# Down weights of the experts loaded as two halves of the partitions, two neighbouring rows to a partition

## The chip, the cores and the metric

The kernel runs on one core of a Trainium2 chip. The metric is the device time of one execution in microseconds (us); lower is better. All numbers of a profile are of one profiled execution.

## The reference

One inference step of a two-layer decoder for a prompt group of 256 tokens and a sample group of 64 tokens (320 in all) with D = 1024. Each layer has a token mixer and then a channel mixer. The first layer's channel mixer is a dense SwiGLU; the second's is a mixture of 8 experts, of which each token uses two. The change touches only the experts:

```python
def _swiglu(h, w_gate, w_up, w_down):
    return (jax.nn.silu(h @ w_gate) * (h @ w_up)) @ w_down
...
    for e in range(N_EXPERTS):
        out = out + combine[..., e:e + 1] * _swiglu(h, w_gate[e], w_up[e], w_down[e])
```

`w_gate[e]` and `w_up[e]` are 1024 x 2816, `w_down[e]` is 2816 x 1024, all float32: 34.6 MB an expert, of which the down weights are 11.5 MB.

## The kernel before, in words

The experts' part begins some 1207 us into the span and ends at 2003 us. It is a row of jobs; a job is one expert with up to 64 tokens (narrow) or up to 128 (wide). In the profiled execution there are eight: job 0 narrow, job 1 "both" (one expert with 192 slots), job 2 narrow, job 3 wide, job 4 narrow, job 5 wide, job 6 narrow, job 7 narrow (the jobs' kinds are fixed in the code; how many follow the seventh is read from the routing).

A job works through 35 pairs of weight tiles. Pairs 0 to 23 are gate and up weights (16 pairs of 2 x 512 KB, then 8 of 2 x 384 KB), pairs 24 to 34 are down weights: 11 pairs, each of two tiles of 128 rows of `w_down` (2 x 512 KB, 1.05 MB). The tiles lie in a ring `MRAW` of seven pairs.

SyncE alone issues these loads (`load_job`, line 551): for each pair it waits until TensorE has used the pair seven places before (`m_used`), then issues two DMAs that both count on the slot's semaphore `m_raw`; so up to seven pairs are loading or wait to be used. In the kernel before, a DMA of a down pair brings one tile of 128 rows: partition p gets row 128 kf + p, 4 KB, for all 128 partitions (lines 568 to 571).

TensorE takes a pair when both its DMAs have landed. A narrow job multiplies the raw tiles (line 2999 for gate and up, line 3017 for down). In a wide job ScalarE first makes a rounded copy (line 1893) and VectorE the remainder (line 1200), and TensorE makes three products (lines 2881 to 2887 and 2906 to 2912). The job for both does the wide and the narrow products of the same weights (lines 2937 to 2952 and 2965 to 2980).

The activations (token x 2816) come out of the gate and up products in six pieces, four of 512 columns and two of 384, into the tile `SG`. `turn` (line 2767) transposes each piece in blocks of 128 columns, so that the columns of the piece lie on the partitions, as the down product needs them: block m of a piece is columns 128 m to 128 m + 127. `turn` is called from `side_pe` and `side_both` between the pairs' matmuls.

Of the kernel before, what the change touches and what calls it, by code (L numbers as in the profile page):

```python
# [28 lines left out]
P = 128  # L29
D = 1024  # L30
# [17 lines left out]
HALF = 64  # L48
# [6 lines left out]
GPAIRS = KD * len(GROUPS)  # L55
PAIRS = GPAIRS + KF // 2
HI_RING, RAW_RING = 5, 7
# [45 lines left out]
def tile_at(t):  # L103

    c0, w = GROUPS[t // 2]
    return (c0 + w * (t % 2)) // P, w // P


def slots_of(side, what):
# [147 lines left out]
def build(nc, a, out):  # L257
    ctx = ExitStack()
    with ctx:
# [35 lines left out]
        MRAW = at("mraw", [P, RAW_RING, 2 * D], F32, RING)  # L295
# [136 lines left out]
        PS = ctx.enter_context(nc.psum_tensor("ps", [P, 8, 512], F32))  # L432
        ident = CF[:, C_ID:C_ID + P]
# [3 lines left out]
        for l in range(DEPTH):  # L437
            for p in PARTS:
                src = {"A": a["w_branch_a"], "B": a["w_branch_b"], "O": a["w_out"]}.get(p, a["w_in"])
# [18 lines left out]
        m_raw = [sem(f"m_raw{n}") for n in range(RAW_RING)]  # L458
# [41 lines left out]
        @block.sync  # L500
        def _(sp):
            def load_pause(s, n):

                l, kind = ADA_GROUPS[PAUSE_GROUPS[s]]
                sp.dma_start(PAUSE[s % 2][n][:, :].unsqueeze(1), ada_src[l][:, n:n + 1, kind * D:(kind + 1) * D])\
                    .then_inc(sem(f"pause_in{n // 4}"), 16)

            def load_unit(n):

                kind, what = UNITS[n]  # L510
                if kind == "ada":
                    g, k = what
                    l, part = ADA_GROUPS[g]
                    src = ada_src[l][:, k:k + 1, part * D:(part + 1) * D]
                else:
                    c, part = what
                    if GU_BASE <= c < DOWN_BASE:
                        i, j = (c - GU_BASE) // 2, (c - GU_BASE) % 2
                        src = (gate_src, up_src)[j][:, 4 * part:4 * part + 4, i * CW:(i + 1) * CW]
                    elif DOWN_BASE <= c < DOWN_BASE + 4:  # L520
                        k = c - DOWN_BASE
                        src = down_src[:, 4 * part:min(4 * part + 4, KF), k * CW:(k + 1) * CW]
                    else:
                        l = 0 if c < GU_BASE else 1
                        p, k = PARTS[(c - 70 * l) // 4], c % 70 % 4 if l == 0 else (c - 70) % 4
                        w, c0 = wide[l, p]
                        src = w[:, 4 * part:4 * part + 4, c0 + k * CW:c0 + (k + 1) * CW]
                if n < KD:
                    sp.dma_start(PAUSE[1][n][:, :].unsqueeze(1), src).then_inc(first_in[n], 16)
                    return  # L530
                if n >= KD + RAW_UNITS:
                    sp.wait_ge(unit_used, n - RAW_UNITS + 1)
                sp.dma_start(RAW[:, n % RAW_UNITS, 0:unit_columns(n)].rearrange("p (k n) -> p k n", k=src.shape[1]),
                             src).then_inc(raw_in[n % RAW_UNITS], 16)

            last = (ENDS[BASE[0, "gb"] + 3], ENDS[DOWN_BASE - 1], ENDS[BASE[1, "gb"] + 3])
            xtm = sem("xtm_in")
            sp.dma_start(XTM[:, 0:2, :], a["x_prompt"][0].rearrange("(t p) d -> p t d", p=P)).then_inc(xtm, 16)
            sp.dma_start(XTM[0:TS, 2, :], a["x_sample"].rearrange("s t d -> (s t) d")).then_inc(xtm, 16)
            for n in range(len(UNITS)):  # L540
                load_unit(n)
                for s in range(3):
                    first = last[s] + RAW_UNITS - 1
                    if n == first and s != 1:
                        sp.wait_ge(sem("on_made"), s // 2 + 1)
                    if first <= n < first + 8:
                        load_pause(s, n - first)

            wg, wu, wd = (a[k][0] for k in ("w_exp_gate", "w_exp_up", "w_exp_down"))

            def load_job(job, e, first=False, both=False):
                g = wg[bass.ds(e, 1)].rearrange("e (k p) n -> p (e k) n", p=P)
                u = wu[bass.ds(e, 1)].rearrange("e (k p) n -> p (e k) n", p=P)
                d = wd[bass.ds(e, 1)].rearrange("e (k p) n -> p (e k) n", p=P)
                for n in range(PAIRS):
                    if not (first and n < RAW_RING):
                        sp.wait_ge(m_used, job * PAIRS + (n - RAW_RING + 1))
                    for j in range(2):
                        if both and n < GPAIRS:
                            (c0, w), k = cols_at(n // 4), 2 * (n % 4)  # L560
                            sp.dma_start(MRAW[:, n % RAW_RING, 2 * w * j:2 * w * (j + 1)].rearrange("p (k n) -> p k n", k=2),
                                         (g, u)[j][:, k:k + 2, c0:c0 + w]).then_inc(m_raw[n % RAW_RING], 16)
                            continue
                        if n < GPAIRS:
                            (c0, w), k = GROUPS[n // KD], n % KD
                            src = (g, u)[j][:, k:k + 1, c0:c0 + 2 * w]
                        else:
                            w, kf = 512, 2 * (n - GPAIRS) + j
                            src = d[:, kf:kf + 1, :]
                        sp.dma_start(MRAW[:, n % RAW_RING, 2 * w * j:2 * w * (j + 1)].unsqueeze(1),  # L570
                                     src).then_inc(m_raw[n % RAW_RING], 16)
                    if first and n == RAW_RING - 1:
                        for i, t in enumerate(HM_TILES):
                            rows = P if t < 2 else TS
                            sp.wait_ge(sem("hm0_out"), i + 1)
                            sp.wait_ge(sem("hm1_out"), i + 1)
                            sp.dma_start(HD[1 + P * t:1 + P * t + rows, :], HMF[0:rows, t, :]).then_inc(hd_stored, 16)

            sp.wait_ge(unit_used, len(UNITS))
            sp.wait_ge(psum_out, CHUNKS)  # L580
            load_job(0, 0, first=True)
            sp.wait_ge(sem("routed"), 1)
            e = sp.value_load(XI[0:1, 1:2], min_val=0, max_val=NE - 1)
            load_job(1, e, both=True)
            with sp.Fori(2, MAIN) as job:
                e = sp.value_load(XI[0:1, bass.ds(job, 1)], min_val=0, max_val=NE - 1)
                load_job(job, e)
            extra = sp.value_load(XI[0:1, 15:16], min_val=1, max_val=1 + EXTRA)
            with sp.Fori(0, 1 + EXTRA) as k:
                with sp.If(k < extra):  # L590
                    e = sp.value_load(XI[0:1, bass.ds(k + MAIN, 1)], min_val=0, max_val=NE - 1)
                    load_job(k + MAIN, e)
            for t in range(2):
                sp.wait_ge(sem("y_out"), 2 * t + 2)
                sp.dma_start(out["yp"][0, P * t:P * t + P, :], XTM[:, t, :]).then_inc(sem("y_stored"), 16)
            sp.wait_ge(sem("y_out"), 2 * TT)
            sp.dma_start(out["ys"].rearrange("s t d -> (s t) d"), XTM[0:TS, 2, :]).then_inc(sem("y_stored"), 16)
            sp.wait_ge(sem("y_stored"), 48)
# [1572 lines left out]
        def _(pe):  # L2171
            M = nc.tensor
# [189 lines left out]
            for d in range(KD):  # L2362
                ins = M.transpose(PS[:, b, d * 16:d * 16 + SEQS], CT[:, d * P:(d + 1) * P], CF[0:SEQS, C_ID:C_ID + SEQS])
# [3 lines left out]
            for k in range(5):  # L2367
                b = aux()
                if k < 4:
                    for d in range(4):  # L2370
                        kd = 4 * (k % 2) + d
                        ins = M.transpose(PS[:, b, d * P:(d + 1) * P], XTM[:, k // 2, kd * P:(kd + 1) * P], ident)
                else:
                    for d in range(KD):
                        ins = M.transpose(PS[:, b, d * TS:(d + 1) * TS], XTM[0:TS, 2, d * P:(d + 1) * P],
                                          CF[0:TS, C_ID:C_ID + TS])
# [23 lines left out]
            for l in range(DEPTH):  # L2400
# [53 lines left out]
                for k in range(4):  # L2454
                    tokens(H1, l)(BASE[l, "i"] + k, k % 2, k)
                    if k == 1:
                        pe.wait_ge(sem("ws_in"), 16 * 10 * (l + 1))
                        b = aux()
                        for g in range(G4):
                            ins = M.transpose(PS[:, b, g * P:(g + 1) * P], WSRR[:, g, :], ident)  # L2460
# [3 lines left out]
                for g in range(G4):  # L2464
                    ins = M.transpose(PS[:, b, g * P:(g + 1) * P], WSR[:, g, :], ident)
                ins.then_inc(aux_in, 1)
                b = aux()
                for g in range(G4):
                    ins = M.transpose(PS[0:TS, b, g * TS:(g + 1) * TS], WSRS[:, g, :], CF[0:TS, C_ID:C_ID + TS])
                ins.then_inc(aux_in, 1)  # L2470

                for k in range(4):
# [8 lines left out]
                    for m in range(2):  # L2481
                        n = 2 * k + m
# [284 lines left out]
            def turn(bank, src, nf):  # L2767

                for m in range(nf):
                    ins = M.transpose(PS[:, bank, m * P:(m + 1) * P], src[:, m * P:(m + 1) * P], ident)  # L2770
                return ins

            def place(bank, marks):
# [314 lines left out]
```

## Time and profile before

| what | value |
|---|---|
| median of 3 runs | 2020.82 us (2020.23 to 2024.37) |
| the profiled execution's own time | 2022.59 us |
| its span, first to last instruction | 2020.7 us |
| TensorE matmul busy | 1908.5 us, 94% |
| VectorE, ScalarE busy | 962.1 us, 741.7 us |
| SyncE's DMA queue | 458.02 MB, 64.1% of 16 DMA engines' span |
| down weights | 176 DMAs of 512 KB, median 12.3 us from issue to landing |

The busy shares are means over stages with different limits: in some of them TensorE never stops, in others it stands still between pairs until a transfer lands. "DMA share" in the windows is the mean busy share of the 16 DMA engines, and GB/s is what they moved; a share can read a little over 1. A transfer that keeps the engines busy and moves few bytes is limited somewhere other than in the number of engines.

### The profile page before, as it was taken

How to read it: one execution, taken by the hardware profiler on the slowest of the kernel's cores; microseconds unless marked ns; L12 is line 12 of the kernel's file. 1: busy time of each engine (PE TensorE's matmuls, PEld its weight loads, DVE VectorE, ACT ScalarE, POOL GpSimd, SP SyncE). 2: the span in 40 equal slices, each digit the busy share in tenths (PEclk: the TensorE clock that was granted, in tenths of full speed). 3: DMA queues.
4: the chain of work that ended last, by engine and by line, in shares of the span. 5: the costliest groups of instructions: out<-in, count | busy, mean ns of one | idle time of the engine just before them, and what ended most of it. 6: DMA issues, size and time to landing. Idle time of an engine off the chain costs nothing. (4 is left out here: it accounts for less than half of the span.)

```text
span 2020.7 us, 31287 instructions
## 1 busy us (share of the span) xinstructions
PE 1908.5 (94%) x12597; PEld 1480.7 (73%) x12597; DVE 962.1 (48%) x1334; ACT 741.7 (37%) x927; POOL 127.0 (6%) x169
## 2 busy tenths in 40 slices
PE   7999999998999989999999988999998999899797
PEld 5999999997999979999998963456534863584233
DVE  4476554556344354765445451355414751783011
ACT  4434324435334344343244331344304641561001
POOL 2100002300000011000022010000000000000000
PEclk9999999999999999999999989999999999999999
DMA  9635356573665636344565459956699899999995
GB/s 356 203 112 164 113 165 181 187 261 94 199 217 194 199 119 201 94 130 126 186 180 166 158 190 408 376 176 230 211 383 406 300 409 407 374 348 407 400 407 233
DMA packets 239096, 488.48 MB, mean 242 GB/s; under 512 B 16919, under 2 KB 145033, under 8 KB 238962
## 3 DMA queue, kind: packets, MB, share of 16 engines
q1 hardware_dynamic: 229504, 458.02, 64.1%
q0 software_dynamic: 9440, 28.50, 4.6%
q8 instruction: 100, 1.64, 0.3%
q14 instruction: 34, 0.28, 0.0%
q10 hardware_dynamic: 18, 0.04, 0.0%
HBM read 473.90 MB, written 12.59 MB: 241 GB/s over the span
## 5 line engine op out<-in xcount | busy, mean ns | idle before, releaser
L614 DVE TENSOR_TENSOR wlo<-raw,whi 128x1024 fp32r<-128x1024 f32 x244 | 289.1, 1212 | 313.5 <-ACT whi L1602 312.3
L2267 PE MATMUL ps<-h1h,whi 128*128 128x320 f32 x1248 | 386.3, 322 | 7.6 <-DVE h1l L721 3.9
L2268 PE MATMUL ps<-h1l,whi 128*128 128x320 f32 x1248 | 371.7, 310 | 0.0
L1602 ACT ACTIVATE whi<-raw 128x1024 fp32r<-128x1024 f32 x244 | 247.8, 1046 | 119.4 <-PE ps L2652 44.8
L2267 PEld LDWEIGHTS ps<-h1h,whi 128*128 128x128 f32 x1248 | 236.2, 189 | 23.7 <-issue 17.2
L2268 PEld LDWEIGHTS ps<-h1l,whi 128*128 128x128 f32 x1248 | 236.4, 189 | 0.1
L2999 PE MATMUL ps<-mraw,xef 128*64 128x512 f32 (+1 forms) x960 | 211.4, 573 | 17.7 <-DMA mraw<-in_w_exp_up 14.7
L2313 PE MATMUL ps<-h1h,wlo 128*128 128x320 f32 x1248 | 209.3, 310 | 0.0
L2313 PEld LDWEIGHTS ps<-h1h,wlo 128*128 128x128 f32 x1248 | 189.0, 188 | 0.4 <-issue 0.4
L1200 DVE TENSOR_TENSOR mlo<-mraw,mhi 128x2048 fp32r<-128x2048 f32 (+1 forms) x70 | 150.1, 2165 | 9.4 <-ACT mhi L1893 9.3
L2999 PEld LDWEIGHTS ps<-mraw,xef 128*64 128x64 f32 x960 | 62.8, 138 | 122.1 <-issue 87.2
L1893 ACT ACTIVATE mhi<-mraw 128x2048 fp32r<-128x2048 f32 (+1 forms) x70 | 127.1, 1820 | 56.3 <-DMA mraw<-in_w_exp_up 29.0
L3017 PE MATMUL ps<-mraw,gtf 128*64 128x512 f32 x440 | 105.7, 604 | 22.2 <-DMA mraw<-in_w_exp_down 20.8
L1224 DVE TENSOR_TENSOR mhi<-mraw,mhi 128x2048 fp32r<-128x2048 f32 (+1 forms) x35 | 75.9, 2169 | 56.8 <-PE ps L2952 32.1
L3017 PEld LDWEIGHTS ps<-mraw,gtf 128*64 128x64 f32 x440 | 27.1, 136 | 87.2 <-DMA mraw<-in_w_exp_down 53.3
L1422 DVE TENSOR_TENSOR gtf<-sgt,ps 128x256 f32<-128x256 f32 (+1 forms) x36 | 14.3, 398 | 157.3 <-ACT sgt L1941 157.3
L1901 ACT ACTIVATE mhi<-mraw 128x2048 fp32r<-128x2048 f32 (+1 forms) x35 | 63.5, 1815 | 68.8 <-PE ps L2952 42.5
L2881 PE MATMUL ps<-mhi,xeh 128*128 128x512 f32 (+1 forms) x192 | 75.5, 393 | 5.5 <-ACT mhi L1893 5.5
L2267 PE MATMUL ps<-h2h,whi 128*128 128x320 f32 x256 | 77.0, 315 | 0.0
L2268 PE MATMUL ps<-h2l,whi 128*128 128x320 f32 x256 | 75.5, 309 | 0.0
L2882 PE MATMUL ps<-mhi,xel 128*128 128x512 f32 (+1 forms) x192 | 72.5, 378 | 0.0
L2005 ACT ACTIVATE sg<-ps 128x512 f32<-128x512 f32 (+1 forms) x30 | 16.9, 562 | 148.9 <-PE ps L2999 148.9
(489 smaller groups left out, 3017.2 us busy)
## 6 DMA issues: line engine op xcount, KB each, us to landing
mraw<-in_w_exp_down SPq DMA_DIRECT2D x176, 512.0 KB, 12.3
raw<-in_w_in SPq DMA_DIRECT2D x128, 512.0 KB, 4.0
mraw<-in_w_exp_gate SPq DMA_DIRECT2D x128, 512.0 KB, 7.0
mraw<-in_w_exp_up SPq DMA_DIRECT2D x128, 512.0 KB, 8.7
raw<-in_w_ada SPq DMA_DIRECT2D x64, 512.0 KB, 3.8
mraw<-in_w_exp_gate SPq DMA_DIRECT2D x64, 384.0 KB, 6.1
mraw<-in_w_exp_up SPq DMA_DIRECT2D x64, 384.0 KB, 8.0
pause<-in_w_ada SPq DMA_DIRECT2D x32, 512.0 KB, 6.4
```

What stands on the lines that cost most here:

```text
L614: V.tensor_tensor(WLO[:, u % RAW_UNITS, 0:w], RAW[:, u % RAW_UNITS, 0:w], WHI[:, h % HI_UNITS, 0:w].bitcast(F32), ALU.subtract).then_inc(l ...
L1200: V.tensor_tensor(MLO[:, n % RAW_RING, 0:w], MRAW[:, n % RAW_RING, 0:w], MHI[:, n % HI_RING, 0:w].bitcast(F32), ALU.subtract).then_inc(m_l ...
L1224: V.tensor_tensor(MHI[:, BOTH_HI + n % BOTH_LO, 0:w], MRAW[:, n % RAW_RING, 0:w], MHI[:, n % BOTH_HI, 0:w].bitcast(F32), ALU.subtract).the ...
L1602: A.activation(WHI[:, h % HI_UNITS, 0:w], RAW[:, u % RAW_UNITS, 0:w], ACT.Copy).then_inc(hi_made, 1)
L1893: A.activation(MHI[:, n % HI_RING, 0:w], MRAW[:, n % RAW_RING, 0:w], ACT.Copy).then_inc(m_hi, 1)
L2267: M.matmul(out_, w, v[0], start=start, stop=False, skip_group_check=True)
L2268: M.matmul(out_, w, v[1], start=False, stop=False, skip_group_check=True)
L2313: ins = M.matmul(PS[:, 2 * j + m, 0:T], w[1][:, s], parts[0][:, k * T:(k + 1) * T], start=False, stop=(k == KD - 1), skip_group_check=True)
L2881: M.matmul(o_, XEH[:, k, :], hi_[:, s], start=(k == 0), stop=False)
L2882: M.matmul(o_, XEL[:, k, :], hi_[:, s], start=False, stop=False)
L2999: ins = M.matmul(PS[HALF * j:HALF * j + HALF, GROUP_BANKS[g][2 * i], 0:w], XEF[:, k, :], MRAW[:, p % RAW_RING, s], start=(k == 0), stop=(k ...
L3017: ins = M.matmul(PS[HALF * h:HALF * h + HALF, DOWN_BANKS[0], :], GTF[:, kf, :], MRAW[:, p % RAW_RING, s], start=(kf == 0), stop=(kf == KF ...
```

## The change

The rows of the down weights are dealt out to the partitions in another order. A group is what one piece of the activations covers: 512 rows (384 in the last two). Of a group, partition p now takes the four (three) neighbouring rows 4p to 4p + 3 (3p to 3p + 2); tile m of the group is row 4p + m on partition p. Two tiles of a pair that lie in one group are thus two neighbouring rows, 8 KB in one piece, on each partition.

Such a pair is still loaded by two DMAs of 512 KB, but each now covers 64 partitions and both tiles: the first partitions 0 to 63, the second partitions 64 to 127. This holds for 10 of the 11 down pairs. The other pair (tiles 18 and 19) lies across two groups and is loaded as before by two DMAs of 128 partitions x 4 KB, now from rows three apart.

`turn` takes every fourth (third) column of the piece for a block, to match. The number of DMAs, of transposes and of matmuls is unchanged, and so are the ring and all waits.

```diff
+def row_of(kf):
+
+    t = kf // 4 if kf < 16 else 4 + (kf - 16) // 3
+    f0, nf = tile_at(t)
+    return f0 * P, nf, kf - f0
...
+            def load_down(e, n, slot, j):
+
+                kf = 2 * (n - GPAIRS)
+                c0, nf, m = row_of(kf)
+                if row_of(kf + 1)[0] == c0:
+                    rows, part = wd[bass.ds(e, 1), c0:c0 + nf * P, :].rearrange("e (p m) n -> p (e m) n", m=nf), slice(HALF * j, HALF * j + HALF)
+                    sp.dma_start(MRAW[part, slot, :].rearrange("p (m n) -> p m n", m=2), rows[part, m:m + 2, :])\
+                        .then_inc(m_raw[slot], 16)
+                    return
+                c0, nf, m = row_of(kf + j)
+                rows = wd[bass.ds(e, 1), c0:c0 + nf * P, :].rearrange("e (p m) n -> p (e m) n", m=nf)
+                sp.dma_start(MRAW[:, slot, D * j:D * (j + 1)].unsqueeze(1), rows[:, m:m + 1, :]).then_inc(m_raw[slot], 16)
...
-                d = wd[bass.ds(e, 1)].rearrange("e (k p) n -> p (e k) n", p=P)
...
-                            w, kf = 512, 2 * (n - GPAIRS) + j
-                            src = d[:, kf:kf + 1, :]
+                            load_down(e, n, n % RAW_RING, j)
+                            continue
...
-                    ins = M.transpose(PS[:, bank, m * P:(m + 1) * P], src[:, m * P:(m + 1) * P], ident)
+                    ins = M.transpose(PS[:, bank, m * P:(m + 1) * P], src[:, m:nf * P:nf], ident)
```

On SyncE, the end of the first job's loads, in the kernel before (`128x1024` is partitions x elements of one DMA; L570 issues all loads of a job):

```order
L570 DMA mraw<-in_w_exp_gate 128x768
L570 DMA mraw<-in_w_exp_up 128x768
L570 DMA mraw<-in_w_exp_down 128x1024 x22
L583 TENSOR_LOAD xi
L583 ISA x2
```

The same place in the changed kernel (L589 is the old L570, L564 and L569 are the two branches of `load_down`):

```order
L589 DMA mraw<-in_w_exp_gate 128x768
L589 DMA mraw<-in_w_exp_up 128x768
L564 DMA mraw<-in_w_exp_down 64x2048 x18
L569 DMA mraw<-in_w_exp_down 128x1024 x2
L564 DMA mraw<-in_w_exp_down 64x2048 x2
L602 TENSOR_LOAD xi
L602 ISA x2
```

Nothing moved: 22 DMAs stand where 22 stood, and 20 of them have half the partitions and twice the bytes on each. On TensorE the order of all instructions is the same; only the read pattern of the transposes differs.

## Rows read from the trace of the kernel before

**Rows 1.** The page: busy tenths of TensorE and DMA, GB/s, in 40 equal slices.
```profile
PE   7999999998999989999999988999998999899797
...
DMA  9635356573665636344565459956699899999995
GB/s 356 203 112 164 113 165 181 187 261 94 199 217 194 199 119 201 94 130 126 186 180 166 158 190 408 376 176 230 211 383 406 300 409 407 374 348 407 400 407 233
```

**Rows 2.** Stages of the jobs: window, us, busy, granted clock, DMA share, GB/s.
```profile
core 0: us, PE busy (x) PEld busy (x) DVE busy (x) ACT busy (x) POOL busy (x), PEclk, DMA share, GB/s
1257.50:1285.00 27.50, 23.38 (x102) 6.73 (x102) 2.09 (x4) 1.86 (x4) 0.00 (x0) 1.00 1.03 406
...
1403.80:1458.60 54.80, 54.80 (x236) 31.00 (x238) 24.21 (x13) 19.10 (x15) 0.00 (x0) 1.00 0.62 214
1458.60:1512.70 54.10, 51.91 (x249) 19.66 (x249) 9.27 (x23) 6.35 (x13) 0.95 (x1) 1.00 0.95 358
...
1544.00:1616.10 72.10, 71.01 (x330) 58.03 (x331) 59.49 (x49) 47.28 (x34) 0.94 (x1) 0.98 0.91 330
1616.10:1648.20 32.10, 32.04 (x149) 25.83 (x147) 26.02 (x15) 20.32 (x16) 0.00 (x0) 1.00 1.03 410
1648.20:1697.60 49.40, 48.24 (x234) 17.25 (x233) 8.61 (x22) 5.78 (x12) 0.94 (x1) 1.00 1.03 406
1698.60:1726.20 27.60, 23.45 (x102) 6.80 (x102) 2.09 (x4) 1.86 (x4) 0.00 (x0) 1.00 1.03 409
1728.90:1800.80 71.90, 70.81 (x330) 58.11 (x331) 61.29 (x49) 48.15 (x34) 0.95 (x1) 0.98 0.92 341
...
1915.70:1971.30 55.60, 51.05 (x233) 17.27 (x233) 7.89 (x20) 4.81 (x11) 0.00 (x0) 0.97 1.03 407
1972.30:2002.70 30.40, 28.84 (x142) 12.84 (x142) 0.71 (x2) 1.43 (x4) 0.00 (x0) 1.00 0.79 315
```

**Rows 3.** TensorE in order of time, in a narrow job's down stage.
```profile
1892.69 1.94 PE L3017 MATMUL ps<-mraw,gtf 128*64 128x512 f32 x8 [0.61 <-DMA mraw<-in_w_exp_down]
1894.56 0.55 PE L2770 MATMUL ps<-cf,sg 128*128 128x128 f32 x3
1895.26 1.94 PE L3017 MATMUL ps<-mraw,gtf 128*64 128x512 f32 x8 [0.15 <-DMA mraw<-in_w_exp_down]
```

**Rows 4.** The page's costliest groups: busy us, mean ns, idle before and releaser.
```profile
L3017 PE MATMUL ps<-mraw,gtf 128*64 128x512 f32 x440 | 105.7, 604 | 22.2 <-DMA mraw<-in_w_exp_down 20.8
...
L3017 PEld LDWEIGHTS ps<-mraw,gtf 128*64 128x64 f32 x440 | 27.1, 136 | 87.2 <-DMA mraw<-in_w_exp_down 53.3
```

**Rows 5.** Windows around transfers at the span's two ends, columns as in rows 2.
```profile
2015.70:2018.20 2.50, 0.00 (x0) 0.00 (x0) 1.71 (x3) 0.00 (x0) 0.00 (x0) 0.50 1.00 403
...
2018.60:2019.60 1.00, 0.00 (x0) 0.00 (x0) 0.00 (x0) 0.00 (x0) 0.00 (x0) 0.50 1.09 238
5.60:8.00 2.40, 2.33 (x11) 2.33 (x12) 0.00 (x0) 1.69 (x2) 0.39 (x6) 1.00 1.02 247
```

**Rows 6.** DMA issues of the whole span: count, KB each, median us to landing.
```profile
mraw<-in_w_exp_down SPq DMA_DIRECT2D x176, 512.0 KB, 12.3
...
out_yp<-xtm SPq DMA_DIRECT2D x2, 512.0 KB, 2.7
...
xtm<-in_x_sample SPq DMA_DIRECT2D x1, 256.0 KB, 7.3
...
out_ys<-xtm SPq DMA_DIRECT2D x1, 256.0 KB, 2.9
```

**Rows 7.** TensorE in order of time, at the start of wide job 3.
```profile
1544.02 0.47 PE L2881 MATMUL ps<-mhi,xeh 128*128 128x512 f32 x1 [2.74 <-ACT mhi L1893]
1544.33 0.39 PE L2882 MATMUL ps<-mhi,xel 128*128 128x512 f32 x1
...
1547.11 0.63 PE L2881 MATMUL ps<-mhi,xeh 128*128 128x512 f32 x1
```

**Rows 8.** Weight loads of the transposes (line 2770): duration ns min/median/max.
```profile
L2770 PEld LDWEIGHTS ps<-cf,sg x198: 137/140/145, 1226.2 to 1982.0; 128*128 128x128 f32 x198
```

## The prediction

> **What bounds the kernel now.** I read the page's slices first, then the windows of each job's stages, then TensorE in order of time within one stage, and last the transfers elsewhere in the program that look like the new ones. The slices show two halves of the program: up to slice 23 the DMA engines are half idle, and in the last 17 most slices run at 370 to 409 GB/s [rows 1]. That last part is the experts, and only there does the change act.
>
> The windows divide it [rows 2]. In the down stage of a narrow job (1257.5, 1698.6; 27.5 us for 11 pairs) the DMA share is 1.03 at 406 to 409 GB/s, while TensorE is busy for 23.4 us. In order of time a pair is eight matmuls in 1.94 us, and one follows the other after 2.56 or 2.57 us (1892.69, 1895.26), with the wait ended by the landing of down weights [rows 3]. 1.0486 MB at 409 GB/s is 2.56 us as well: transfers set this pace. The wait stands in the group of line 3017 too, 53.3 us of its weight loads' idle time and 20.8 us of its matmuls' [rows 4]. So narrow down stages are bound by transfers, and whatever a down transfer gains or loses comes through there. The gate stages of narrow jobs are nearly bound by them too: share 1.03 in 1648.2 and 1915.7, 0.95 in job 2's [rows 2]. Wide jobs are bound by TensorE, by little: 32.1 us for 11 down pairs are 2.92 us each against 2.56, and the gate stages' share is 0.91 and 0.92. Only the job for both has real room: 54.8 us for 11 pairs are 4.98 us each, at a share of 0.62.
>
> **The change, the loads.** Neither the bytes nor the number of DMAs changes. What changes is that 20 of the 22 DMAs of a job write 64 partitions instead of 128. The trace holds three transfers to set beside each other. At the end of the span two stores of 128 partitions (y of the prompt, 512 KB each) run at share 1.00 and 403 GB/s. Right behind them one store of 64 partitions (y of the samples, 256 KB), with nothing beside it, has the share 1.09 and 238 GB/s [rows 5]; it takes 2.9 us to land where 512 KB take 2.7 [rows 6]. The engines are as busy and move about half. Near the start the load of the samples (64 partitions, 256 KB) lies in a window with share 1.02 and 247 GB/s [rows 5], though other small loads share that window; so it is no matter of stores alone. All 16 engines work on a transfer of 64 partitions, each at half its rate, as if two of them shared one way into the memory.
>
> The price: per unit of share the lone store moves 238 / 1.09 = 218 GB/s. A DMA of 524 KB at that rate takes 2.40 us, a pair of two 4.81 us instead of 2.56 us. Both ends: 247 GB/s gives 4.25 us. At the other end, if two DMAs of opposite halves that stand behind each other in the queue could fill each other's gaps, the pair costs 2.56 us and nothing is lost. I take 4.81: each engine must finish its share of the lower half before it starts on the upper, all 16 start together, and the store is the only row with nothing beside it. The extra is 2.25 us a pair and 22.5 us for the ten pairs of a job.
>
> The Trainium skill has a rule that bears on the two halves together, which no row here shows ("SBUF — State Buffer", section "Can I just issue two DMAs to hit both halves?"): two concurrent DMAs, one at partition 0 and one at partition 64, were only 6% faster than a single one, "they serialize". The table of the section before it ("Door 1: The DMA port swizzle") gives 196 GB/s for partitions 0 to 63; an estimate by that figure is 5.35 us a pair and a sum some 40 us larger than mine. The rows' 238 and 218 GB/s agree in kind.
>
> **The sum over the jobs.** Where transfers set the pace the whole 22.5 us is felt; where the DMA engines stood idle before, that idle time is used up first. Idle time is 1 minus share / 1.03.
> Job 0 (narrow, transfers bind): 22.5.
> Job 1 (both): 4.81 us a pair is below TensorE's 4.98: 0. The cover is thin; at 5.35 us it would cost 4 us.
> Job 2 (narrow behind the one for both): share 0.95 over 54.1 us leaves 4.2 us: 22.5 - 4.2 = 18.3.
> Jobs 3 and 5 (wide): share 0.91 over 72.1 us leaves 8.4, share 0.92 over 71.9 us leaves 7.7: 14.1 and 14.8. Part of it falls into the next job's gate stage, as the ring is then empty instead of full.
> Jobs 4 and 6 (narrow behind wide, share 1.03 throughout): 22.5 each.
> Job 7 (last, narrow): its down stage was 30.4 us with share 0.79, as TensorE's work at the end set 2.9 us of it: 22.5 - 2.9 = 19.6.
> Sum: 134.3 us.
>
> **The clock.** In narrow down stages TensorE will work 1.94 of 4.81 us. At job 3's start an idle stretch of 2.74 us was followed by matmuls of 0.63 us where they had taken 0.39 [rows 7], and the stage's mean granted clock is 0.98 [rows 2], so 0.02 x 72.1 = 1.4 us of it is the price of one such start. At half the clock (1.2 instead of 2.4 GHz) a down pair would take up to 3.9 us, still below 4.81, so within the stage it is hidden. The start of the next stage pays once; two of the five already do. I put 3 us, between 0 and 7 (five starts by 1.4).
>
> **The change, the transposes.** The same 198 weight loads of 140 ns [rows 8] now read every fourth or third column. No row shows such a load. Below: 0, as the count is the same and they lie beside matmuls. Above: each takes twice as long, and matters only where TensorE binds: jobs 3 and 5 have 22 each and job 1 has 44, so 88 x 0.14 = 12.3 us. In narrow jobs it would vanish in the waits. The row nearest is the 140 ns of the plain load; I take 0.
>
> SyncE issues the same number of DMAs behind the same waits, and ScalarE, VectorE and TensorE read the same places of the ring, at no cost.
>
> **Total.** 134.3 + 3 = 137 us. The profiled execution took 2022.6 us, so it would be 2160; the median of the runs is 1.8 us below it, so 2158 us. With both upper ends of clock and transposes it is 2174, and with a rate 10% lower (5.3 us a pair) near 2195.
>
> **Rivals.**
> *The halves slip against each other.* If of two engines that share a way one runs ahead by half a transfer, each is alone half of the time: (2.56 + 4.81) / 2 = 3.69 us a pair, 11.3 us a job. Less the same idle times: 11.3 + 0 + 7.1 + 2.9 + 11.3 + 3.6 + 11.3 + 8.4 = 56 us, so 2077 us. For it: the queue is never empty in these stages, so a lead once gained can last. Against it: a pair of tiles is ready only when the slowest engine is done, and an engine that has caught up waits for the next issue, where all start together again.
>
> *Full rate, and the longer pieces help (the other side).* The place is the same ten pairs. If lower and upper halves overlap fully, nothing is lost, and a partition's 8 KB in one piece could carry less overhead. The best rate over 2 us or more in the rows is 410 GB/s against 406 to 409 in the narrow stages [rows 2]; even 3% would be 0.08 us a pair, 4 us for the 50 pairs of the five narrow jobs and some 1 us in the wide ones: 2016 us, between 2012 and 2021. It decides from the point where a pair of halves takes less than 2.56 us. Against it stands the lone store at 238 GB/s. The Trainium skill speaks for it ("Perfetto Trace Analysis", section "DMA Optimizations"): putting small transfers together into larger ones, its examples go up to 8 KB, is its first advice where transfers bind. No row here shows a piece of 8 KB, and the 4 KB pieces run at 409 GB/s already.
>
> *The change does not do what it says.* If the 8 KB pieces are cut into 4 KB again, only the halving of the partitions is left; the forecast stays.
>
> **How the numbers follow.** The forecast with its unknown costs (2115 to 2195) gets 0.76; the slipping halves (2040 to 2115) 0.12; full rate 0.11; what I have not thought of 0.01. The range 2070 to 2195 leaves out full rate and the lower part of the slipping halves, some 2 in 10 with the misses at the top. A difference under 0.2% (4 us) can't be told from none: the full rate splits into faster 0.06 and same 0.05. Slower has 0.89.
>
> **What would show it.** Right: narrow down stages (27.5 us before) last near 50 us, with a DMA share still near 1.03 and GB/s near 225; the down DMAs' time to landing roughly doubles; the job for both keeps its 54.8 us; wide down stages grow to about 40 us; the transposes' loads stay at 140 ns. Gate stages keep 406 to 409 GB/s wherever gate weights alone are moving. Wrong: a down stage at 400 GB/s or more (full rate), or near 300 with stages of about 40 us (slipping halves); or the job for both longer by more than a few us, or loads of the transposes near 280 ns.

## The result, and the profile after

The changed kernel takes 2193.7 us (median of 4 runs, 2180.04 to 2200.43) against 2022.12 us before (4 runs): ratio 1.0837, 95% interval [1.0795, 1.0878]. The forecast was 2158 us in a range of 2070 to 2195, so the direction and the main mechanism came true and the size was some 35 us short. The median lies 1.3 us under the upper end of the range, and two of the four runs (2195.67 and 2200.43 us) lie above it. The profiled execution took 2191.74 us, its span is 2189.9 us.

The slices of the page after, to set against [rows 1]:

```profile
PE   7999999999999899999998869999698868986776
...
DMA  9634456736666463346654897698999999899995
GB/s 339 213 96 150 146 181 193 241 97 197 198 203 199 129 183 105 112 139 182 199 193 170 329 245 251 173 240 331 238 339 241 360 289 321 255 316 343 309 333 145
```

A slice is now 54.7 us long instead of 50.5. The first 22 slices are the part ahead of the experts, which did not change. Behind them the DMA engines are as busy as before, but slices at 238 to 255 GB/s stand between those at 289 to 360. The windows of the stages say which they are (columns as in [rows 2]; for each job the gate stage and the down stage):

```profile
1208.10:1261.50 53.40, 47.46 (x231) 18.91 (x231) 8.38 (x39) 6.63 (x13) 1.91 (x2) 0.97 0.95 347
1263.10:1313.20 50.10, 32.09 (x102) 8.48 (x102) 2.09 (x4) 1.86 (x4) 0.00 (x0) 0.80 1.02 245
...
1432.40:1487.20 54.80, 54.80 (x236) 31.18 (x236) 24.21 (x13) 19.11 (x15) 0.00 (x0) 1.00 0.87 239
1487.20:1542.20 55.00, 52.27 (x250) 20.27 (x249) 9.27 (x23) 6.35 (x13) 0.95 (x1) 1.00 0.95 338
1545.00:1595.20 50.20, 32.72 (x102) 8.21 (x102) 2.09 (x4) 1.86 (x4) 0.00 (x0) 0.77 1.01 246
1597.90:1670.00 72.10, 71.87 (x329) 58.75 (x329) 58.29 (x47) 45.51 (x32) 0.95 (x1) 0.96 0.91 302
1670.30:1720.20 49.90, 39.07 (x147) 27.30 (x148) 27.67 (x16) 21.68 (x18) 0.00 (x0) 0.93 1.01 258
1720.20:1777.00 56.80, 49.85 (x234) 17.38 (x233) 8.62 (x22) 5.77 (x12) 0.95 (x1) 1.00 1.03 384
1779.90:1828.70 48.80, 33.95 (x102) 8.67 (x102) 2.09 (x4) 1.86 (x4) 0.00 (x0) 0.72 1.02 255
1831.40:1904.40 73.00, 72.47 (x329) 59.14 (x329) 58.29 (x47) 45.48 (x33) 0.95 (x1) 0.95 0.89 294
1904.40:1952.50 48.10, 39.20 (x149) 27.41 (x149) 27.67 (x16) 21.68 (x18) 0.00 (x0) 0.93 1.01 261
...
2017.40:2063.10 45.70, 28.83 (x102) 7.91 (x102) 0.71 (x2) 1.43 (x4) 0.00 (x0) 0.85 1.01 260
2063.50:2124.90 61.40, 52.56 (x233) 17.82 (x233) 7.91 (x20) 5.03 (x11) 0.00 (x0) 0.95 1.03 370
2126.20:2171.40 45.20, 34.29 (x142) 13.97 (x142) 0.71 (x2) 1.43 (x4) 0.00 (x0) 0.89 0.83 194
```

A narrow down stage takes 45.7 to 50.2 us instead of 27.5, at a DMA share of 1.01 to 1.02 and 245 to 260 GB/s (the last job's, which was 30.4 us long, takes 45.2). A wide one takes 49.9 and 48.1 us instead of 32.1 and 31.7. The job for both keeps its 54.8 us; only its share rose from 0.62 to 0.87. In order of time, TensorE in job 2's down stage (compare [rows 3]):

```profile
1544.99 3.63 PE L3036 MATMUL ps<-mraw,gtf 128*64 128x512 f32 x8 [2.74 <-DMA mraw<-in_w_exp_down]
1549.56 1.94 PE L3036 MATMUL ps<-mraw,gtf 128*64 128x512 f32 x8 [0.94 <-DMA mraw<-in_w_exp_down]
1554.11 2.54 PE L3036 MATMUL ps<-mraw,gtf 128*64 128x512 f32 x8 [2.61 <-DMA mraw<-in_w_exp_down]
1556.58 0.91 PE L2789 MATMUL ps<-cf,sg 128*128 128x128 f32 x3
1558.66 3.64 PE L3036 MATMUL ps<-mraw,gtf 128*64 128x512 f32 x8 [1.16 <-DMA mraw<-in_w_exp_down]
```

A pair now follows after 4.55 to 4.57 us instead of 2.56. Some pairs take 3.6 us instead of 1.94 at a lower clock (the stage's mean granted clock is 0.77), still within that time. The groups of the page after, to set against [rows 4], and the down weights' time to landing against [rows 6]:

```profile
L3036 PE MATMUL ps<-mraw,gtf 128*64 128x512 f32 x440 | 142.0, 781 | 89.0 <-DMA mraw<-in_w_exp_down 89.0
...
L3036 PEld LDWEIGHTS ps<-mraw,gtf 128*64 128x64 f32 x440 | 31.8, 160 | 176.5 <-DMA mraw<-in_w_exp_down 131.0
...
mraw<-in_w_exp_down SPq DMA_DIRECT2D x176, 512.0 KB, 22.1
```

The wait for down weights is 89.0 us before the matmuls where it was 20.8, and landing takes 22.1 us where it took 12.3. The transposes' weight loads did get slower: 209 ns where [rows 8] had 140.

```profile
L2789 PEld LDWEIGHTS ps<-cf,sg x198: 188/209/230, 1227.2 to 2141.5; 128*128 128x128 f32 x198
```

### The profile page after: what moved, and what is told of

It is laid out like the page before. It is cut to its first block, busy times and chain, and to the rows that moved or that the text cites. A ratio compares the mean times of both kernels' runs of the same rounds, so it can differ in the third digit from the quotient of the medians.

```text
span 2189.9 us, 31287 instructions
## 1 busy us (share of the span) xinstructions
PE 1974.1 (90%) x12597; PEld 1496.2 (68%) x12597; DVE 962.8 (44%) x1334; ACT 741.3 (34%) x927; POOL 127.3 (6%) x169
## 3 DMA queue, kind: packets, MB, share of 16 engines
q1 hardware_dynamic: 219264, 458.02, 67.4%
## 4 chain that ended last, share of the span: by engine, by line
PE 25%; DMA 21%; DVE 1%; issue 1%; ACT 1%; SPq 1%; DVEq 0%; ACTq 0%
DMA mraw<-in_w_exp_down 14%; DMA mraw<-in_w_exp_up 6%; PE ps L3018 5%; PE ps L2956 2%; PE ps L2900 2%; PE ps L2906 2%; PE ps L2901 2%; PE ps L3036 1%; PE ps L2964 1%; PE ps L2286 1%; PE ps L2984 1%; PE ps L2965 1%; PE ps L2287 1%; PE ps L2971 1%; PE ps L2332 1%
## 5 line engine op out<-in xcount | busy, mean ns | idle before, releaser
L3036 PE MATMUL ps<-mraw,gtf 128*64 128x512 f32 x440 | 142.0, 781 | 89.0 <-DMA mraw<-in_w_exp_down 89.0
L3036 PEld LDWEIGHTS ps<-mraw,gtf 128*64 128x64 f32 x440 | 31.8, 160 | 176.5 <-DMA mraw<-in_w_exp_down 131.0
## 6 DMA issues: line engine op xcount, KB each, us to landing
mraw<-in_w_exp_down SPq DMA_DIRECT2D x176, 512.0 KB, 22.1
```

The costliest lines, as they stand in the source:

```text
L3036: ins = M.matmul(PS[HALF * h:HALF * h + HALF, DOWN_BANKS[0], :], GTF[:, kf, :], MRAW[:, p % RAW_RING, s], start=(kf == 0), stop=(kf == KF ...
```

## The experiments

Two theories of the loss stood against each other first. W: 64 neighbouring partitions are reached by half as many ways as 128, so two DMA engines share one. P: it is the new pieces (8 KB long, or 12 and 16 KB apart from one partition to the next) that read slowly. A third, N, came with e4: any DMA of 64 partitions is slow, whichever they are. The four kernels below ran on one chip, beside the kernel before at 2023.05 us.

**e1, the new order of rows without the halves.**

```diff
-                if row_of(kf + 1)[0] == c0:
+                if False:
```

> New order of rows and transposes as in the changed kernel, but every down DMA covers 128 partitions x 4 KB (rows three or four apart). Theory W (64 neighbouring partitions are reached by half as many ways, two DMA engines share one): the whole loss is gone, narrow down stages 27.5 us at 409 GB/s; what is left is the slower weight loads of the transposes (209 instead of 140 ns, 88 of them where TensorE binds, 6 us): 2020 to 2030 us. Theory P (the pieces' distance of 12 or 16 KB slows the reads): near 2190 us.

2023.43 us, ratio 0.9997 [0.9985, 1.0009]. The first narrow down stage:

```profile
1259.70:1287.20 27.50, 23.51 (x102) 7.01 (x102) 2.09 (x4) 1.86 (x4) 0.00 (x0) 1.00 1.03 406
```

Order and distance of the rows cost nothing that shows: the interval is -3 to +2 us. Nor do the slower weight loads, which this kernel has as well (median 208 ns): the 6 us expected of them did not show in the total.

**e2, one DMA of 128 partitions x 8 KB.**

```diff
-                    rows, part = wd[bass.ds(e, 1), c0:c0 + nf * P, :].rearrange("e (p m) n -> p (e m) n", m=nf), slice(HALF * j, HALF * j + HALF)
-                    sp.dma_start(MRAW[part, slot, :].rearrange("p (m n) -> p m n", m=2), rows[part, m:m + 2, :])\
-                        .then_inc(m_raw[slot], 16)
+                    rows = wd[bass.ds(e, 1), c0:c0 + nf * P, :].rearrange("e (p m) n -> p (e m) n", m=nf)
+                    if j:
+                        return
+                    sp.dma_start(MRAW[:, slot, :].rearrange("p (m n) -> p m n", m=2), rows[:, m:m + 2, :])\
+                        .then_inc(m_raw[slot], 32)
```

> As the changed kernel, but a pair in one group is one DMA of 1 MB, 128 partitions x 8 KB, that counts 32. Theory W: no loss, 2015 to 2030 us, down stages at 409 to 420 GB/s; pieces of 8 KB may gain up to 3% of the down transfers (4 to 5 us against the kernel with 4 KB pieces). Theory P (pieces of 8 KB or their distance are slow): near 2190 us.

2018.76 us, ratio 0.9981 [0.9969, 0.9993]: the whole loss is gone, and there is a gain of some 4 us, close to the noise. Two windows inside narrow down stages (the stages last 26.9 us):

```profile
1253.50:1279.50 26.00, 22.61 (x102) 6.82 (x98) 2.09 (x4) 1.86 (x4) 0.00 (x0) 1.00 1.02 415
1509.00:1535.00 26.00, 22.62 (x102) 6.83 (x98) 2.09 (x4) 1.86 (x4) 0.00 (x0) 1.00 1.01 418
```

**e3, halves alone.** The kernel before with its own order of rows and its own transposes; only the split of a down pair is the new one, in pieces of 4 KB.

```diff
-                            w, kf = 512, 2 * (n - GPAIRS) + j
-                            src = d[:, kf:kf + 1, :]
+                            kf, part = 2 * (n - GPAIRS), slice(HALF * j, HALF * j + HALF)
+                            sp.dma_start(MRAW[part, n % RAW_RING, :].rearrange("p (k n) -> p k n", k=2),
+                                         d[part, kf:kf + 2, :]).then_inc(m_raw[n % RAW_RING], 16)
+                            continue
```

> The kernel before with its old order of rows and plain transposes; only the split of a down pair changes: two DMAs of 64 partitions (0 to 63, 64 to 127) x two pieces of 4 KB, for all 11 pairs. Theory W: slow as the changed kernel, 2175 to 2215 us (11 pairs instead of 10, no slower weight loads). Theory P: 2020 to 2025 us.

2191.04 us, ratio 1.0851 [1.0823, 1.0879]. The halves alone make the whole loss:

```profile
1257.70:1306.00 48.30, 31.80 (x102) 8.22 (x102) 2.09 (x4) 1.86 (x4) 0.00 (x0) 0.79 1.03 237
```

**e4, 64 partitions, but every second one.**

```diff
-                    rows, part = wd[bass.ds(e, 1), c0:c0 + nf * P, :].rearrange("e (p m) n -> p (e m) n", m=nf), slice(HALF * j, HALF * j + HALF)
+                    rows, part = wd[bass.ds(e, 1), c0:c0 + nf * P, :].rearrange("e (p m) n -> p (e m) n", m=nf), slice(j, P, 2)
```

> As the changed kernel (two DMAs of 64 partitions x 8 KB), but the first takes the even partitions and the second the odd ones. Theory W (it matters which partitions a DMA writes, since only neighbouring 64 crowd onto half the ways): all or nearly all of the loss is gone, 2015 to 2040 us. Rival N (any DMA of 64 partitions is slow, whichever they are): near 2190 us.

2018.11 us, ratio 0.998 [0.9967, 0.9994]. The number of DMAs is that of the changed kernel, each is again 64 partitions x 8 KB, and the stage runs at full rate (a window inside a stage of 27.0 us):

```profile
1259.50:1285.50 26.00, 22.52 (x102) 6.82 (x98) 2.09 (x4) 1.85 (x4) 0.00 (x0) 1.00 1.02 414
```

So it is not how many partitions a DMA writes but which: theory N falls, W holds in each of the four. That the shared thing is a way from two engines into the same partitions is the explanation that fits; what the runs show is the dependence on the set of partitions.

The pieces of the transfers say it directly. The trace has a duration for each, and a piece of 8 KB takes 576 ns in the changed kernel (median) and 309 ns in e4.

One thing changes along with the partitions in e4: its DMAs read rows spread over 2 MB of memory, those of the changed kernel rows within 1 MB. No run changes the partitions alone. A theory that blames the narrower stretch of memory has the kernel before against it, whose DMAs read 0.5 MB in one stretch at 406 to 409 GB/s, and e3, whose halves read two such stretches of 0.25 MB each and are slow.

The second four ask for the 35 us that the sum was short. They ran on another chip, beside the kernel before at 2025.31 us. Theory "credit" is the prediction's: the DMA engines' idle time is used up first. Its rival is "full price": that idle time is there because the ring is full, and the lead of seven pairs is what the next job already lives on.

**e5 and e6, halves only in the wide, or only in the narrow jobs.**

```diff
-                if row_of(kf + 1)[0] == c0:
+                if halves and row_of(kf + 1)[0] == c0:
...
-            with sp.Fori(2, MAIN) as job:
-                e = sp.value_load(XI[0:1, bass.ds(job, 1)], min_val=0, max_val=NE - 1)
-                load_job(job, e)
+            for job in range(2, MAIN):
+                e = sp.value_load(XI[0:1, job:job + 1], min_val=0, max_val=NE - 1)
+                load_job(job, e, halves=(job % 2 == 1))
```

(for e6 `== 0`, and the first and last jobs too; the rest of the edit hands `halves` on to `load_down`. The loop over jobs is written out for it on SyncE. No run has that alone; in e5 the narrow down stages without halves last 27.5 to 27.6 us, as before.)

> Of the changed kernel's half-partition DMAs only those of the wide jobs 3 and 5 are left; all other down DMAs cover 128 partitions x 4 KB. Credit theory (the prediction's sum: the idle time of the DMA engines in the gate stage before is used up first): 14.1 + 14.8 = 29 us over the kernel before, about 2052 us. Rival, full price (that idle time is there because the ring of seven pairs is full, and the next job already lives on those seven): 2 x 22.5 = 45 us and a few for the clock, about 2068 to 2074 us.

> Only the narrow jobs 0, 2, 4, 6 and 7 have half-partition DMAs. Credit theory: 22.5 + 18.3 + 22.5 + 22.5 + 19.6 = 105 us, about 2128 us. Full price: 5 x 22.5 - 2.9 = 110 us, and with a clock cost above the 3 us forecast some 10 us more, 2133 to 2145 us. If narrow and wide jobs add up, this one's loss and that of the run with wide jobs alone make the changed kernel's 170 us, less what the two share.

e5: 2066.24 us, ratio 1.0219 [1.0194, 1.0245], 41 us over the kernel before (some 5 us either way): near the 45 of full price, clear of the 29 of credit. Job 3 and the narrow job behind it, in e5:

```profile
1539.00:1612.10 73.10, 72.17 (x329) 59.11 (x330) 58.70 (x48) 46.32 (x33) 0.94 (x1) 0.95 0.93 315
1612.10:1659.40 47.30, 36.59 (x150) 24.98 (x148) 27.50 (x16) 21.18 (x16) 0.00 (x0) 1.00 1.01 258
1659.40:1714.60 55.20, 49.93 (x234) 17.36 (x233) 8.61 (x22) 5.77 (x12) 0.94 (x1) 1.00 1.03 407
```

The gate stage's share is 0.93 where [rows 2] has 0.91: the idle time was hardly used. The down stage is 15.2 us longer, and the gate stage behind it 5.8 us, although its own transfers run at 407 GB/s: it starts without its lead. Together 21 us for one wide job, against 14 with credit. What SyncE waits for during the wide gate stage, in the kernel before (1544 to 1616.1) and in the changed one (1597.9 to 1670):

```profile
SPq L570 <- PE ps L2887: 47.5, 22, 9.0
...
SPq L589 <- PE ps L2906: 42.2, 17, 8.8
```

That is 47.5 and 42.2 us of waiting until TensorE has used a pair, which is a full ring.

e6: 2139.35 us, ratio 1.0563 [1.0534, 1.0592], 114 us over the kernel before, between full price's 110 and 120. The two add up to 155 us of the changed kernel's 164 on this chip; with some 5 us of uncertainty in each of the three, the 9 us that are missing are not clear of noise.

**e7, filler for the clock, and e8, the changed kernel once more.** Behind the down pairs stand matmuls whose result nobody reads, so that TensorE does not stand idle:

```diff
+                    if GPAIRS + 4 <= p < PAIRS - 1:
+                        warm(4, 1)
...
+                    if GPAIRS <= p < PAIRS - 1 and not by_marks and side is not SIDE_FIRST:
+                        warm(5, 1)
```

(first the wide jobs, then the narrow ones)

> The changed kernel with work that has no use for TensorE behind each down pair: five matmuls of 128x320 (1.6 us) in the narrow jobs but the first and the last, four in the last pairs of wide jobs. They fit into the waits for transfers. Theory C (the low clock after those waits costs 12 to 15 us in the stages behind them, instead of the 3 us forecast): granted clock back to 0.98, 8 to 14 us faster than the changed kernel, 2180 to 2186 us. Rival (the clock costs what was forecast): within 3 us of the changed kernel, or slower by the filler.

> The changed kernel once more, as the measure for the others on this chip: 2180 to 2200 us, a granted clock near 0.96.

e7: 2193.96 us, ratio 1.0845 [1.0819, 1.0872]; e8: 2189.26 us, 1.0795 [1.077, 1.082]. The mean granted clock rose from 0.955 (e8) to 0.974 (e7), and the time did not fall. Job 4 of e7, gate and down stage:

```profile
1725.20:1776.30 51.10, 48.48 (x234) 17.84 (x233) 8.62 (x22) 5.78 (x12) 0.94 (x1) 1.00 1.03 387
1779.20:1831.80 52.60, 52.56 (x202) 25.55 (x202) 2.09 (x4) 1.86 (x4) 0.00 (x0) 0.97 1.02 258
```

and of e8:

```profile
1717.50:1775.50 58.00, 50.60 (x234) 17.41 (x233) 8.61 (x22) 5.77 (x12) 0.94 (x1) 0.99 1.03 384
1778.10:1825.70 47.60, 31.24 (x102) 8.24 (x102) 2.09 (x4) 1.85 (x4) 0.00 (x0) 0.79 1.01 238
```

With filler the gate stage is 6.9 us shorter, but it began 7.7 us later, and both end within 1 us of each other (1776.3 and 1775.5), at a DMA share of 1.03. In the down stage the filler takes TensorE to 52.56 us busy of 52.6 and the stage is 5 us longer: there it has become a load of its own. In the profiled executions (2195.6 and 2195.5 us) the three narrow down stages with filler are 12 us longer together than in e8, and the rest of the program is as much shorter, so the total can't say what the clock costs. It shows only that keeping TensorE busy in this way gains nothing.

The stages that TensorE binds say more. A lower clock can cost time where TensorE is busy throughout. The wide gate stages are such stages (71.87 us busy of 72.1), and they come right behind the slow narrow down stages. In the changed kernel they take 72.1 and 73.0 us at a granted clock of 0.96 and 0.95, where they took 72.1 and 71.9 at 0.98 [rows 2]; the gate stage of the job for both takes 117.5 us instead of 117.1. That is 1 to 2 us in all.

## Why the prediction was right, and where it was short

*What bounds.* Right. Down stages bound by transfers took the loss, the job for both hid it: 171.8 us before, 172.3 after.

*The rate of the halves.* Right within some per cent, and this is the step that carried the forecast. The lone store of 64 partitions gave 4.81 us a pair, an extra of 2.25. The page's queue line gives nearly the same afterwards:

```profile
q1 hardware_dynamic: 219264, 458.02, 67.4%
```

67.4% of 2189.9 us are 1476 us; before it was 64.1% of 2020.7, 1295 us. The 181 us more, over 80 pairs, are 2.26 us a pair. Not all of it is in the pairs themselves. The pieces of 8 KB add up to 4.57 us a pair (365.2 us of all 16 engines' time for the 80 pairs, against 207.9 in e4), which is near the 4.55 us between pairs; a piece takes 1.86 times as long, not twice. Another 14 us are in the experts' pieces of 4 KB, which e4 moves in 308.8 us and the changed kernel in 322.8. Why a half takes less than double, and why its neighbours take longer, no run shows. As a forecast of the total the rival of slipping halves (2077 us) is out, and full rate (2016 us) is near what e2 and e4 measured (2019 and 2018 us) once the neighbouring halves were gone.

*The sum over the jobs.* Here it failed: "where the DMA engines stood idle before, that idle time is used up first". For that idle time it took off 4.2, 8.4 and 7.7 us, and 2.9 us in job 7. Measured in the profiled executions, from the first matmul of a job to that of the next (job 7: to its last):

| job | before | after | more | forecast |
|---|---|---|---|---|
| 0 narrow | 79.5 | 106.8 | 27.3 | 22.5 |
| 1 both | 171.8 | 172.3 | 0.5 | 0 |
| 2 narrow | 85.5 | 110.7 | 25.2 | 18.3 |
| 3 wide | 104.1 | 122.3 | 18.2 | 14.1 |
| 4 narrow | 80.7 | 111.2 | 30.5 | 22.5 |
| 5 wide | 103.5 | 121.0 | 17.5 | 14.8 |
| 6 narrow | 83.3 | 111.0 | 27.7 | 22.5 |
| 7 narrow | 87.0 | 107.9 | 20.9 | 19.6 |

Sum 167.8 us against 134.3. The wide gate stages kept their idle time (share 0.91 and 0.89 after, 0.91 and 0.92 before), since SyncE waits there for a place in the ring and can't load further ahead; e5 shows it alone. Job 2's gate stage kept its own as well (share 0.95 before and after), and its 25.2 us stand against a forecast of 18.3. Job 7's 2.9 us rest on something else, TensorE's work at the end, and 20.9 against 19.6 does not speak against them. The prediction's signs show the fault too: it expected wide down stages of about 40 us, and they took 49.9 and 48.1. With nothing taken off the sum is 157.5 us.

Of the 10 us left, the trace accounts for most. Added up over all transfers, the DMA engines are busy 164 us longer in the seven jobs other than job 1, which is 7 us more than seven times 22.5. Their idle time in these jobs grew by 3 us, where the sum had counted on 23 us less of it. Part of the idle time may be at the starts of narrow down stages, where TensorE now waits up to 2.9 us behind the gate stage (1777.0 to 1779.9) where it waited 1.0; that link is not shown.

*The range.* That it held is partly luck. Its upper end came from a rate 10% lower, which is not what happened, and with the upper ends of clock and transposes added on top it would have been some 2212 us. The other rate that the prediction names, 5.35 us a pair, would have come nearer in the total (some 2198 us) with a pair time further off than 4.81 is from the 4.55 measured.

*The clock.* 3 us were put down. The granted clock fell to 0.72 to 0.80 in the first three narrow down stages and to 0.85 and 0.89 in the last two, and it is hidden there, as said. Where TensorE binds, 1 to 2 us show, within the forecast's 0 to 7.

*The transposes.* The sign was wrong, since each load took 209 ns and not 140. The cost of 0 was right for the total, by e1. The last job's down stage, which TensorE's own work lengthens, took 32.0 us in e1's profile and 31.8 in e2's and e4's, where the kernel before has 30.4; that these 1.5 us come from the loads is not shown.

## What to carry to other kernels

Before splitting a load in two, look at which partitions each part covers: stages with DMAs of 64 neighbouring partitions ran at 237 to 260 GB/s where 128 partitions, or every second of them, ran at 406 to 418. A single small transfer of the same shape elsewhere in the trace, with its DMA share beside its GB/s, gave the rate beforehand (4.81 us a pair against 4.57). And idle time of a queue in front of a full ring is no reserve: the lead that the ring holds is already part of the next stage's time, and here none of it came off the cost.

## What was not expected of the hardware

Weight loads of a transpose whose columns stand three or four elements apart took 208 to 209 ns (median) instead of 140, at no cost that shows in the total. Pieces of 8 KB instead of 4 KB took a narrow down stage from 27.5 to 26.9 us in the first four of e2's five narrow jobs, and e2 and e4, whose common difference from e1 is the length of the pieces, are the fastest kernels of this study, 0.2% below the one before. The Trainium skill ("Perfetto Trace Analysis", section "DMA Optimizations") advises to put small transfers together into larger ones, and 8 KB is the largest of its examples. The traces agree: 414 to 418 GB/s against 406 to 411.
